# Where the SBUF tiles of a two-block transformer kernel begin: ring, activations and small tiles moved to other start addresses

## The chip, the cores and the metric

The kernel runs on one core of one Trainium2 chip. The metric is the device time of one execution in microseconds (us), the median of several runs. A core has TensorE (matmuls), VectorE, ScalarE and GpSimd, and queues that issue DMAs between HBM and the on-chip memory SBUF. SBUF has 128 partitions; a tile has one start address, the same in every partition, in bytes from the partition's beginning.

## The reference

The program computes two blocks on 256 tokens of width 2048, all in fp32. Cut to what matters:

```python
def first_block(x, ...):            # two layers
    for l in range(2):
        h = rms_norm(x, norm_g[l]); proj = h @ w_in[l]              # 2048 -> 6208
        o_a = diff_attention(q_a, k_a, v_a) ; o_a = rms_norm(o_a) * silu(z_a)
        q_b = rms_norm(c_q) @ w_uq[l]; kv = rms_norm(c_kv) @ w_ukv[l]
        o_b = mla_attention(q_b, kv, rope keys) * silu(z_b)
        x = x + concat(o_a, o_b) @ w_out[l]                         # 2048 -> 2048
    return rms_norm(x)

def second_block(x, mem, ...):      # one layer
    z = rms_norm(x) @ w_in                                          # 2048 -> 3584
    conv_out, pool_out, att = conv(z), pool(z), cross_attention(z, rms_norm(mem) @ w_kv)
    x = x + concat(conv_out, pool_out, att) @ w_out
    u = causal_dwconv(rms_norm(x) @ w_up, ffn_conv_w) + ffn_conv_b  # 2048 -> 11264
    x = x + (silu(gate) * val) @ w_down                             # 5632 -> 2048
    return rms_norm(x)
```

## The kernel before

Nearly all the work is products of a 256-token activation with large weight matrices that come from HBM once. The weights pass in 656 units of 1,024 columns per partition (512 KB; two of them per layer are half as wide) through a ring of four slots. Per unit:

- SP loads it into `stage` (`load`, L292), as soon as the remainder of the unit four before is done;
- ScalarE rounds it to fp32r, the format in which TensorE takes a matmul in one pass, into `w_hi` (`round_unit`, L299);
- VectorE writes what the rounding left, `stage - w_hi`, into `w_lo` (`rest_unit`, L304);
- TensorE multiplies with three products, high x high, high x low and low x high. Round and remainder run three units ahead of TensorE (`LEAD`).

The activations lie split in the same way, high and low half side by side, in `xT`, `mT` (attention and mixer outputs) and `act_T` (FFN).

There are two forms of product. `product_rows` (L326 to L328) holds a 128x128 block of the activation as weights in the array and streams 512 columns of `w_hi` or `w_lo`: 12 matmuls a unit, for all products but the two below. `product_cols` (L344 to L348) holds a 128x128 block of `w_hi` or `w_lo` and streams `xT`: a 256-column matmul with the low weights and a 512-column one with the high weights, 16 a unit. It serves the second block's in-projection (56 units) and the FFN's up-projection (22 turns of 8 units). The heads' transposes, scores and outputs are small fp32 matmuls in the other four PSUM banks (`aux`), written by hand in between the units. Every wait is on a semaphore; the order on each engine is the order of the code.

Where tiles lie is set by the order of their declarations alone. `sb(name, shape)` puts a tile behind the last one, its size rounded up to a multiple of 32 bytes, from address 16,512 on (16,384 bytes of DMA scratch and four constants of 32 bytes stand below). Three stacks share the upper part in time: `b1` (first block) and `b2` (second block) both start behind `bias`, and the FFN's tiles start where `mT` had started.

Of the kernel before, what the change touches and what calls it, by code (L numbers as in the profile page):

```python
# [28 lines left out]
P = 128  # L29
SEQ = 256  # L30
T = SEQ // P
D = 2048
KT = D // P
LAYERS = 2
# [3 lines left out]
HEADS = 8  # L38
# [28 lines left out]
TAPS = 3  # L67
# [28 lines left out]
FFN_ROWS = 2 * FT  # L96
# [67 lines left out]
def build(nc, dram, out):  # L164
# [12 lines left out]
    with ctx:  # L177
        def sb(name, shape, dt=F32, stack=ctx):
            return stack.enter_context(nc.sbuf_tensor("sb_" + name, shape, dt))
# [2 lines left out]
            return ctx.enter_context(nc.semaphore(name))  # L182


        ident = sb("ident", [P, P])
        par_ffn = sb("par_ffn", [P, TAPS + 1, FFN_ROWS])
        stage = sb("stage", [P, RING, UNIT])
        w_hi = sb("w_hi", [P, RING, UNIT], F32R)
        w_lo = sb("w_lo", [P, RING, UNIT], F32R)
        x = sb("x", [P, T, D])  # L190
        xT = sb("xT", [P, KT, 2, SEQ], F32R)
        par = sb("par", [P, G_ALL])
        turn_f32 = sb("turn_f32", [P, 2, 512])
        qkT = turn_f32[:, 1, :]
        sumsq_x = sb("sumsq_x", [P, T, 4])
# [2 lines left out]
        newton_v = sb("newton_v", [P, 16])  # L198
        newton_t = sb("newton_t", [P, 16])
        junk = sb("junk", [P, 512], BF16)  # L200
        sumsq_o = sb("sumsq_o", [P, HEADS * T])
        rstd_o = sb("rstd_o", [P, HEADS * T])
        sumsq_m = sb("sumsq_m", [P, T, 4])
        gain_c = sb("gain_c", [P, 8])
        neg_lam = sb("neg_lam", [P, LAYERS])


        acc = ctx.enter_context(nc.psum_tensor("acc", [P, 4, 512], F32))
# [264 lines left out]
        b1 = lambda name, shape, dt=F32: sb(name, shape, dt, block1)  # L473
# [9 lines left out]
        krT = b1("krT", [P, SEQ])  # L483
        s = b1("s", [P, 3 * SEQ])
        pT = b1("pT", [P, 3 * P])
        lam_l = b1("lam_l", [P, 1])
        neg_max = b1("neg_max", [P, 4])
        row_sum = b1("row_sum", [P, 4])
        inv_sum = b1("inv_sum", [P, 4])
        mix_f = b1("mix_f", [P, 2])  # L490
        sumsq_c = b1("sumsq_c", [P, 4])
        rstd_c = b1("rstd_c", [P, 4])
        sumsq_m2 = b1("sumsq_m2", [P, T])
        rstd_m = b1("rstd_m", [P, T])
        dots = b1("dots", [P, 2 * LAYERS])
# [45 lines left out]
        gfin = ffn_tmp[:, :, :, :].rearrange("p a c t -> p (a c t)")  # L541
        rb3 = sb("rb3", [P, T, P])
        rbc3 = sb("rbc3", [P, SEQ])
        act_T = sb("act_T", [P, FT, 2, SEQ], F32R)
        taps = sb("taps", [P, TAPS + 1, 2, 2])


        U2 = U_MEM + LAYERS * U_LAYER
# [1380 lines left out]
```

How the kernel before makes its waits and increments, by code:

```python
            def __call__(self, ins):  # L272
                self.n += 1
                ins.then_inc(self.semaphore, 1)
                self.eng.wait_ge(self.semaphore, self.base + self.n)
# [10 lines left out]
        def load(sp, base, j, src, n):  # L286
            if not (isinstance(base, int) and base + j < RING):
                sp.wait_ge(lo_ready, base + (j - RING + 1))
            k = src.shape[1]
            dst = stage[:, j % RING, 0:k * n].rearrange("p (k n) -> p k n", n=n)
            sp.dma_start(dst, src).then_inc(staged[j % RING], 16)
# [1 line left out]
        def round_unit(act, quads, j, size=UNIT):  # L294
            act.wait_ge(staged[j % RING], quads * 16 + (j // RING + 1) * 16)
            if not (isinstance(quads, int) and 4 * quads + j < RING):
                act.wait_ge(unit_used, quads * 4 + (j - RING + 1))
            act.activation(w_hi[:, j % RING, 0:size], stage[:, j % RING, 0:size], ACT.Copy).then_inc(hi_ready, 1)
# [1 line left out]
        def rest_unit(dve, base, j, size=UNIT):  # L301
            dve.wait_ge(hi_ready, base + (j + 1))
            dve.tensor_tensor(w_lo[:, j % RING, 0:size], stage[:, j % RING, 0:size],
                              w_hi[:, j % RING, 0:size].bitcast(F32), ALU.subtract).then_inc(lo_ready, 1)
# [5 lines left out]
        def product_rows(pe, base, j, lhs, k0, nk, n, pair, first, last, before_tile1=None):  # L311
            pe.wait_ge(lo_ready, base + (j + 1))
            slot = j % RING
            hi = w_hi[:, slot, 0:nk * n].rearrange("p (k n) -> p k n", n=n)
```

## Time and profile before

| | us |
|---|---|
| median of 3 runs | 2006.61 |
| lowest and highest run | 2005.53, 2006.81 |
| the profiled execution, its own time | 2005.53 |
| its span, first to last instruction | 2003.7 |

The mean granted TensorE clock of that span is 0.996. The profile's columns: PE is TensorE's matmuls, PEld its weight loads (which overlap them), DVE is VectorE, ACT ScalarE, POOL GpSimd, SP the queue that issues most loads. The ends of matmuls are modelled, so a busy TensorE is not one at its peak; the spacing of matmuls is a better measure than the length of one. Line numbers are those of the kernel before.

### The profile page before, as it was taken

The page shows a single profiled execution, that of the slowest core. Times are in us where ns is not written, and L with a number is a line of the kernel's source. Part 1 is how long each engine was busy: PE and PEld are TensorE (multiplying, and loading weights), DVE is VectorE, ACT ScalarE, POOL GpSimd, SP SyncE. Part 2 cuts the span into 40 slices and gives each one's busy share as a digit, 9 for nine tenths or more (in the row PEclk, how much of TensorE's full clock was granted, in tenths as well). Part 3 has the DMA queues.
Part 4 walks back from the last instruction along what each step waited for, and adds up shares of the span by engine and source line. Part 5 has one row for each costly group of instructions (what it writes and reads, how often), then busy time and mean ns, then how long its engine had stood idle before and what let it go on. Part 6 is the DMA issues. An engine that isn't in the chain of part 4 may idle for free.

```text
span 2003.7 us, 28710 instructions
## 1 busy us (share of the span) xinstructions
PE 1969.7 (98%) x9884; PEld 1646.0 (82%) x9884; DVE 1286.8 (64%) x1793; ACT 1028.3 (51%) x1496; POOL 46.3 (2%) x72
## 2 busy tenths in 40 slices
PE   8999999999999999999999999999999999999997
PEld 6788887888888887788888888888888888888886
DVE  6655665655654665555677775787877778754543
ACT  5533675554433565654454544555555555544442
POOL 1000003000000003000100000000000000000000
PEclk9999999999999999999999999999999999999999
DMA  8666544545566545445665545555555555565553
GB/s 282 209 191 196 149 144 130 148 148 177 177 204 191 157 149 158 145 130 186 209 192 172 166 163 189 184 184 183 188 186 186 183 188 188 185 213 191 196 191 125
DMA packets 245653, 357.36 MB, mean 178 GB/s; under 512 B 15238, under 2 KB 134368, under 8 KB 245036
## 3 DMA queue, kind: packets, MB, share of 16 engines
q1 hardware_dynamic: 243916, 349.35, 55.0%
q0 software_dynamic: 1632, 6.67, 1.0%
q8 instruction: 58, 0.95, 0.2%
q14 instruction: 47, 0.39, 0.1%
HBM read 352.82 MB, written 3.16 MB: 178 GB/s over the span
## 4 chain that ended last, share of the span: by engine, by line
PE 93%; issue 4%; POOL 2%; DVE 1%; DMA 0%; ACT 0%; SPq 0%; POOLq 0%; DVEq 0%; ACTq 0%
PE acc L348 20%; PE acc L326 18%; PE acc L328 18%; PE acc L327 18%; PE acc L347 10%; PE aux L403 2%; PE acc L344 1%; PE aux L816 1%; PE aux L815 1%; PE acc L345 1%; DMA sb_kz<-mem 0%; PE aux L778 0%; POOL sb_kz L684 0%; PE aux L797 0%; PE aux L981 0%
## 5 line engine op out<-in xcount | busy, mean ns | idle before, releaser
L304 DVE TENSOR_TENSOR sb_w_lo<-sb_stage,sb_w_hi 128x1024 fp32r<-128x1024 f32 x656 | 801.5, 1224 | 536.2 <-ACT sb_w_hi L299 528.4
L299 ACT ACTIVATE sb_w_hi<-sb_stage 128x1024 fp32r<-128x1024 f32 x656 | 690.8, 1056 | 640.9 <-PE acc L328 368.3
L348 PE MATMUL acc<-sb_xT,sb_w_hi 128*128 128x512 f32 x1740 | 616.5, 398 | 0.0
L347 PE MATMUL acc<-sb_xT,sb_w_lo 128*128 128x256 f32 x1740 | 490.2, 282 | 0.0
L348 PEld LDWEIGHTS acc<-sb_xT,sb_w_hi 128*128 128x128 f32 x1740 | 326.9, 188 | 77.3
L347 PEld LDWEIGHTS acc<-sb_xT,sb_w_lo 128*128 128x128 f32 x1740 | 328.6, 189 | 2.6
L326 PE MATMUL acc<-sb_w_hi,sb_xT 128*128 128x512 f32 x768 | 307.6, 401 | 0.9 <-issue 0.9
L327 PE MATMUL acc<-sb_w_lo,sb_xT 128*128 128x512 f32 x768 | 300.2, 391 | 0.0
L328 PE MATMUL acc<-sb_w_hi,sb_xT 128*128 128x512 f32 x768 | 300.1, 391 | 0.0
L326 PE MATMUL acc<-sb_w_hi,sb_mT 128*128 128x512 f32 x560 | 225.3, 402 | 0.0
L328 PE MATMUL acc<-sb_w_hi,sb_mT 128*128 128x512 f32 x560 | 218.9, 391 | 0.0
L327 PE MATMUL acc<-sb_w_lo,sb_mT 128*128 128x512 f32 x560 | 218.9, 391 | 0.0
L326 PEld LDWEIGHTS acc<-sb_w_hi,sb_xT 128*128 128x128 f32 x768 | 144.9, 189 | 32.1 <-issue 1.6
L328 PEld LDWEIGHTS acc<-sb_w_hi,sb_xT 128*128 128x128 f32 x768 | 144.7, 188 | 31.0
L327 PEld LDWEIGHTS acc<-sb_w_lo,sb_xT 128*128 128x128 f32 x768 | 145.0, 189 | 28.0 <-issue 0.2
L326 PE MATMUL acc<-sb_w_hi,sb_act_T 128*128 128x512 f32 x352 | 136.9, 389 | 0.0
L327 PE MATMUL acc<-sb_w_lo,sb_act_T 128*128 128x512 f32 x352 | 136.9, 389 | 0.0
L328 PE MATMUL acc<-sb_w_hi,sb_act_T 128*128 128x512 f32 x352 | 136.9, 389 | 0.0
L326 PEld LDWEIGHTS acc<-sb_w_hi,sb_mT 128*128 128x128 f32 x560 | 105.6, 189 | 23.3 <-issue 1.0
L328 PEld LDWEIGHTS acc<-sb_w_hi,sb_mT 128*128 128x128 f32 x560 | 105.4, 188 | 23.1
L327 PEld LDWEIGHTS acc<-sb_w_lo,sb_mT 128*128 128x128 f32 x560 | 105.6, 189 | 20.1
L1813 DVE SCALAR_TENSOR_TENSOR sb_ffn_tmp<-sb_ffn_tmp,sb_taps 128x254 f32<-128x254 f32 (+1 forms) x176 | 77.3, 480 | 1.6
(248 smaller groups left out, 1574.9 us busy)
## 6 DMA issues: line engine op xcount, KB each, us to landing
sb_stage<-w_in SPq DMA_DIRECT2D x248, 512.0 KB, 3.8
sb_stage<-w_up SPq DMA_DIRECT2D x176, 512.0 KB, 3.4
sb_stage<-w_out SPq DMA_DIRECT2D x96, 512.0 KB, 3.6
sb_stage<-w_down SPq DMA_DIRECT2D x88, 512.0 KB, 4.4
sb_stage<-w_kv SPq DMA_DIRECT2D x16, 512.0 KB, 6.1
sb_stage<-w_ukv SPq DMA_DIRECT2D x16, 512.0 KB, 3.5
sb_stage<-w_uq SPq DMA_DIRECT2D x12, 512.0 KB, 3.6
sb_kz<-mem SPq DMA_DIRECT2D x4, 512.0 KB, 10.4
```

Source lines behind the costliest of these rows:

```text
L299: act.activation(w_hi[:, j % RING, 0:size], stage[:, j % RING, 0:size], ACT.Copy).then_inc(hi_ready, 1)
L304: dve.tensor_tensor(w_lo[:, j % RING, 0:size], stage[:, j % RING, 0:size], w_hi[:, j % RING, 0:size].bitcast(F32), ALU.subtract).then_inc( ...
L326: pe.matmul(o, x_hi, hi[:, k, :], start=first and k == 0, stop=False)
L327: pe.matmul(o, x_hi, lo[:, k, :], start=False, stop=False)
L328: mm = pe.matmul(o, x_lo, hi[:, k, :], start=False, stop=last and k == nk - 1)
L344: pe.matmul(o, hi[:, k, cols], both, start=True, stop=False)
L345: mm = pe.matmul(o[:, 0:SEQ], lo[:, k, cols], xT[:, k0 + k, 0, :], start=False, stop=False)
L347: pe.matmul(o[:, 0:SEQ], lo[:, k, cols], xT[:, k0 + k, 0, :], start=False, stop=False)
L348: mm = pe.matmul(o, hi[:, k, cols], both, start=False, stop=last and k == 3)
L403: mm = pe.transpose(aux[:, bank, i * P:(i + 1) * P], src(i), ident[:, :])
L815: pe.matmul(o, qkT[:, q * P:(q + 1) * P], qkT[:, 2 * P:2 * P + keys], start=True, stop=False)
L1813: last = dve.scalar_tensor_tensor(out=y[:, k, d:SEQ], in0=sum3[:, k, 0:SEQ - d], scalar=taps[:, 2 - d, half, k:k + 1], in1=y[:, k, d:SEQ], ...
```

## The change

The declarations are written in another order, and five small tiles go to another stack. No instruction is added, removed or moved on any engine: engine by engine (TensorE, VectorE, ScalarE, GpSimd, SP) the rows of the two programs are the same, except that line numbers of the helpers are lower by five. What differs is the start addresses in them.

```diff
-        ident = sb("ident", [P, P])
-        par_ffn = sb("par_ffn", [P, TAPS + 1, FFN_ROWS])
         stage = sb("stage", [P, RING, UNIT])
         w_hi = sb("w_hi", [P, RING, UNIT], F32R)
         w_lo = sb("w_lo", [P, RING, UNIT], F32R)
         x = sb("x", [P, T, D])
         xT = sb("xT", [P, KT, 2, SEQ], F32R)
+        ident = sb("ident", [P, P])
         par = sb("par", [P, G_ALL])
+        par_ffn = sb("par_ffn", [P, TAPS + 1, FFN_ROWS])
         turn_f32 = sb("turn_f32", [P, 2, 512])
...
-        sumsq_o = sb("sumsq_o", [P, HEADS * T])
-        rstd_o = sb("rstd_o", [P, HEADS * T])
-        sumsq_m = sb("sumsq_m", [P, T, 4])
-        gain_c = sb("gain_c", [P, 8])
-        neg_lam = sb("neg_lam", [P, LAYERS])
...
+        neg_lam = b1("neg_lam", [P, LAYERS])
         lam_l = b1("lam_l", [P, 1])
+        gain_c = b1("gain_c", [P, 8])
...
+        sumsq_o = b1("sumsq_o", [P, HEADS * T])
+        rstd_o = b1("rstd_o", [P, HEADS * T])
...
+        sumsq_m = b1("sumsq_m", [P, T, 4])
...
+        taps = sb("taps", [P, TAPS + 1, 2, 2])
         act_T = sb("act_T", [P, FT, 2, SEQ], F32R)
-        taps = sb("taps", [P, TAPS + 1, 2, 2])
```

The start addresses that follow, each with what is left over past a multiple of 2,048 bytes:

| tile | before | past 2,048 | after | past 2,048 |
|---|---|---|---|---|
| ident | 16,512 | 128 | 114,816 | 128 |
| par_ffn | 17,024 | 640 | 115,904 | 1,216 |
| stage | 18,432 | 0 | 16,512 | 128 |
| w_hi | 34,816 | 0 | 32,896 | 128 |
| w_lo | 51,200 | 0 | 49,280 | 128 |
| x | 67,584 | 0 | 65,664 | 128 |
| xT | 83,968 | 0 | 82,048 | 128 |
| par | 116,736 | 0 | 115,328 | 640 |
| turn_f32 | 117,312 | 576 | 117,312 | 576 |
| mT, ffn_tmp | 122,880 | 0 | 122,656 | 1,824 |
| bias | 155,648 | 0 | 155,424 | 1,824 |
| qa (first tile of `b1`) | 163,840 | 0 | 163,616 | 1,824 |
| s (`b1`) | 224,288 | 1,056 | 224,064 | 832 |
| zT | 170,016 | 32 | 169,792 | 1,856 |
| mkv | 198,688 | 32 | 198,464 | 1,856 |
| mkT | 206,880 | 32 | 206,656 | 1,856 |
| act_T | 133,120 | 0 | 132,960 | 1,888 |
| taps | 223,232 | 0 | 132,896 | 1,824 |

All starts after are multiples of 32; `stage`, `w_hi`, `w_lo`, `x` and `xT` are multiples of 128, and `mT` and `act_T` are 32 past a multiple of 64. The distances among `stage`, `w_hi`, `w_lo`, `x` and `xT` stay as they were.

## Rows read from the trace of the kernel before

**Rows 1.** Page, span and busy time: us, share of the span, instructions.

```profile
span 2003.7 us, 28710 instructions
...
PE 1969.7 (98%) x9884; PEld 1646.0 (82%) x9884; DVE 1286.8 (64%) x1793; ACT 1028.3 (51%) x1496; POOL 46.3 (2%) x72
```

**Rows 2.** Page, part 4: the chain that ended last, by engine.

```profile
PE 93%; issue 4%; POOL 2%; DVE 1%; DMA 0%; ACT 0%; SPq 0%; POOLq 0%; DVEq 0%; ACTq 0%
```

**Rows 3.** Windows, two stretches: span, busy us (instructions) by engine, PEclk, DMA share, GB/s.

```profile
1355.00:1395.00 40.00, 40.00 (x229) 34.74 (x228) 30.83 (x43) 22.11 (x28) 0.00 (x0) 1.00 0.60 190
1800.00:1850.00 50.00, 50.00 (x222) 41.43 (x221) 24.52 (x23) 21.00 (x23) 0.00 (x0) 1.00 0.57 191
```

**Rows 4.** Groups by shape: busy us, mean ns | idle us before, releasers.

```profile
L304 DVE TENSOR_TENSOR sb_w_lo<-sb_stage,sb_w_hi 128x1024 fp32r<-128x1024 f32 x652 | 798.7, 1227 | 535.3 <-ACT sb_w_hi L299 528.2 <-DVE sb_rstd_m L449 0.3
L299 ACT ACTIVATE sb_w_hi<-sb_stage 128x1024 fp32r<-128x1024 f32 x652 | 688.3, 1058 | 640.9 <-PE acc L328 368.3 <-PE acc L348 267.5 <-DMA sb_stage<-w_in 3.0
...
L347 PEld LDWEIGHTS acc<-sb_xT,sb_w_lo 128*128 128x128 f32 x1740 | 328.6, 189 | 2.6
L348 PEld LDWEIGHTS acc<-sb_xT,sb_w_hi 128*128 128x128 f32 x1740 | 326.9, 188 | 77.3
L326 PE MATMUL acc<-sb_w_hi,sb_xT 128*128 128x512 f32 x768 | 307.6, 401 | 0.9 <-issue 0.9
...
L326 PE MATMUL acc<-sb_w_hi,sb_mT 128*128 128x512 f32 x560 | 225.3, 402 | 0.0
L328 PE MATMUL acc<-sb_w_hi,sb_mT 128*128 128x512 f32 x560 | 218.9, 391 | 0.0
...
L326 PE MATMUL acc<-sb_w_hi,sb_act_T 128*128 128x512 f32 x352 | 136.9, 389 | 0.0
...
L328 PE MATMUL acc<-sb_w_hi,sb_act_T 128*128 128x512 f32 x352 | 136.9, 389 | 0.0
```

**Rows 5.** Groups by shape: the small fp32 products, transposes first.

```profile
L403 PE MATMUL aux<-sb_ident,sb_x 128*128 128x128 f32 x128 | 19.1, 271 | 0.0
...
L778 PE MATMUL aux<-sb_ident,sb_s 128*128 128x128 f32 x96 | 15.6, 271 | 0.0
...
L815 PE MATMUL aux<-sb_turn_f 128*128 128x256 f32 x32 | 9.5, 380 | 0.0
...
L999 PE MATMUL aux<-sb_mkT,sb_zT 128*128 128x256 f32 x16 | 4.1, 379 | 0.0
```

**Rows 6.** Groups by shape, VectorE: product with a broadcast row.

```profile
L1805 DVE TENSOR_TENSOR sb_ffn_tmp<-sb_ffn_tmp,sb_rbc 128x512 f32<-128x512 f32 x44 | 30.5, 692 | 1.5
...
L1713 DVE TENSOR_TENSOR sb_zT<-sb_sum,sb_rbc 128x512 f32<-128x512 f32 x9 | 6.2, 692 | 0.3
```

**Rows 7.** DMA issues: KB each, median us from issue to landing.

```profile
sb_stage<-w_up SPq DMA_DIRECT2D x176, 512.0 KB, 3.4
sb_stage<-w_out SPq DMA_DIRECT2D x96, 512.0 KB, 3.6
sb_stage<-w_down SPq DMA_DIRECT2D x88, 512.0 KB, 4.4
...
mem_kv<-sb_qa POOLq DMA_DIRECT2D x1, 1024.0 KB, 5.2
...
sb_mkv<-mem_kv POOLq DMA_DIRECT2D x1, 1024.0 KB, 5.4
```

**Rows 8.** Timeline, one turn of the ring: start us, us, instruction, idle before.

```profile
500.82 1.23 DVE L304 TENSOR_TENSOR sb_w_lo<-sb_stage,sb_w_hi 128x1024 fp32r<-128x1024 f32 x1 [1.43 <-ACT sb_w_hi L299]
...
502.21 3.09 SPq L292 DMA_DIRECT2D sb_stage<-w_out  x2
...
510.61 1.06 ACT L299 ACTIVATE sb_w_hi<-sb_stage 128x1024 fp32r<-128x1024 f32 x1 [0.29 <-PE acc L328]
```

**Rows 9.** Waits: engine and line, what for, us in total, times, longest.

```profile
ACT sb_w_hi L299 <- DMA sb_stage<-w_in: 3.0, 1, 3.0
```

**Rows 10.** The chain in order of time, its start: start us, us, what.

```profile
2.53 9.67 DMA sb_kz<-mem
```

## Prediction

> **What bounds the kernel now.** I read the page's busy times first, then the chain of waits, then two steady stretches by window, then the groups of instructions by shape, and last the waits and the loads. TensorE is busy for 1969.7 of 2003.7 us, 98%, against 64% for VectorE and 51% for ScalarE [rows 1], and it carries 93% of the chain that ended last [rows 2]. So the time is, nearly, the number of matmuls times the spacing between them. The two steady stretches show that spacing [rows 3]: in the FFN's up-projection 229 matmuls in 40 us, 175 ns each or 349 ns for a pair of one 256-column and one 512-column product; in the down-projection 222 in 50 us, 225 ns each. The granted clock is 1.00 in both, the upper of its two levels.
>
> This change adds, removes and moves no instruction. It moves tiles in SBUF. The question is therefore one: does a stream, a weight load, a vector or scalar pass or a transfer take longer or shorter from another start address? The rows of before can answer part of it, because this kernel already has tiles at awkward starts: ident stands at 16,512 (128 bytes past a multiple of 2,048, where the ring goes), s at 224,288, zT at 170,016 and mkv at 198,688, each 32 bytes past a multiple of 64, while x, xT, mT, act_T, ffn_tmp and the ring stand at multiples of 2,048.
>
> **The change part by part.**
>
> TensorE, 8,752 large matmuls. 5,040 of them are product_rows (L326 to L328: 768 + 560 + 352 rows of each of three lines [rows 4]); there the moving operand is w_hi or w_lo, whose starts go from a multiple of 2,048 to 128 bytes past one, and the weights are xT (the same shift), mT and act_T (to 32 bytes past a multiple of 64). 3,712 are product_cols: 232 units (56 of the in-projection, 176 of the FFN) of 16. There w_hi and w_lo are the weights and xT moves. What does the address cost? Compare like with like [rows 5]. A 128x256 matmul on turn_f32, a multiple of 64, takes 380 ns (L815); on mkT and zT, both 32 bytes past a multiple of 64, 379 ns (L999). A transpose of x, a multiple of 2,048, takes 271 ns; of s, 271 ns (L778); both read ident at 128 past a multiple. The differences are 0 and -1 ns. These are fp32 products and not the fp32r of the large ones, and the ends of matmuls are modelled, so I take them as the nearest rows and not as proof. The value I take is 0 ns. The ends: one ns either way is what such rows can't tell, -8.8 to +8.8 us over 8,752; upward I keep 7 ns on the row products as well, worked out under the slower rival, +35 us.
>
> Weight loads. They run beside the matmuls. For 1740 pairs of product_cols the two loads take 189 + 188 ns and the load side sat idle for 77.3 + 2.6 us, 46 ns a pair [rows 4]. A load that grows by less than 23 ns disappears there. In product_rows the load of 188 or 189 ns stands in a spacing of 225 ns, so 36 ns cover it. Cost 0, and the cover is those two numbers.
>
> VectorE and ScalarE. The round to w_hi (1058 ns) and the remainder (1227 ns) follow one another within a unit, and in the down-projection a unit of 12 matmuls lasts 12 x 225 = 2.7 us, so neither is near its limit; the two sat idle for 535 and 641 us before these instructions [rows 4]. From rows, the address costs them nothing either: the same 128x512 product with a broadcast row takes 692 ns into ffn_tmp at a multiple of 2,048 and 692 ns into zT at 32 past a multiple of 64 [rows 6]. Even 10% on both, 0.23 us a unit, would be covered by the ring, whose remainder is made three units ahead of its use. Cost 0.
>
> The loads. Each 512 KB load writes rows of 2 KB (1 KB for the narrow units) to a start that was a multiple of 2,048 and is now 128 past one. Landing takes 3.4 us for w_up [rows 7]. How much is spare is read from one turn of the ring [rows 8]: VectorE's remainder ends at 500.82 + 1.23 = 502.05, the load into that slot goes out at 502.21, and ScalarE rounds it four units on, at 510.61: 8.4 us, while a w_out load lands in 3.6 us [rows 7], under half of it. In all the run ScalarE waited once for a stage load, 3.0 us [rows 9]. From one row on the other side: the load into mkv, at an odd start, lands in 5.4 us, and the store of the same 1024 KB from qa, at a multiple of 2,048, in 5.2 [rows 7]. So steady transfers cost 0; what remains is the opening, where the chain rests for 9.67 us on the load of mem [rows 10]. I give it +0.2 us (the 4% between 5.4 and 5.2 on half of 9.67 us, the rest being latency); the ends are 0 and +2 us, the latter if all of the 9.67 us grew by a fifth, which is how far loads of one size already differ (w_down lands in 4.4 us, w_out in 3.6 [rows 7]).
>
> The Trainium skill has a rule that speaks against the change. "DMA: Bandwidth & Descriptors", section "How a descriptor splits into AXI transactions", says that a descriptor is cut at every 256 bytes, that one which starts off such a boundary begins with a partly used transaction, and gives the beats. It speaks of reads; if it held for the SBUF side of a load as well, a 2 KB row at 128 past a boundary would by that page need 9 transactions and 68 beats in place of 8 and 64, a 1 KB row 36 in place of 32. By that rule, and as an estimate from the page's beats, loads would take 6 to 12% longer. No row here shows a 2 KB row at such a start, so the trace neither agrees nor disagrees. On the rows above it would make the opening about 1 us longer and leave the rest covered, 2008 us, which is still no change, so it has no chance of its own.
>
> Small tiles (par, par_ffn, taps, the sums and the rstd values) are read by instructions of some 160 to 690 ns on engines that have idle time. Cost 0.
>
> The sum: 0 (TensorE) + 0 (loads of weights) + 0 (VectorE, ScalarE) + 0.2 (opening) on a span of 2003.7 and an execution of 2005.53, thus 2005.7 for the profiled execution. The median of the runs stands 1.1 above that execution, so the forecast is 2006.8 us for the median: no change.
>
> **The rivals.**
>
> Slower, because TensorE's moving rows no longer begin on a boundary. The place is product_rows. A 512-column row of 2 KB is 32 pieces of 64 bytes; if a start 128 bytes off costs one piece more, each of 5,040 matmuls takes 225/32 = 7 ns more, 35 us, and the time is 2042. It decides from 0.8 ns a matmul on, since 5,040 x 0.8 is 4 us. The column products would gain nothing and lose nothing: one eighth of a 512-byte weight row is 24 ns a load, 47 a pair, against the 46 of cover. For it speaks that the row products are the tightest loop and that their fp32r streams have no row at an odd start. Against it: rows 5, and the transposes in particular, which read ident at the very offset in question. Chance 8%.
>
> Slower, because the queues run full. The DMA share is 0.60 and 0.57 in the two steady stretches [rows 3]. Loads bind the kernel only when packets take 1/0.60 = 1.67 times as long. If writes off a boundary took twice as long, the shares would be 1.20 and 1.14, and most of the run would stretch by 10 to 20%: some 2250 us. Short of that there is the mild form, a few us at the opening and at changes of stage, 2011 to 2015, where a fifth more on each load is no longer covered at four or five of them. Together 5%.
>
> Faster, because a clash of equal starts goes. If two operands that begin at the same place in a 2,048-byte frame disturbed one another, moving them apart would help. xT and w_hi keep their distance of 49,152 bytes, so nothing changes there. mT against w_hi goes from 88,064 (a multiple of 2,048) to 89,760 (not one). L326 on mT takes 402 ns and on act_T 389; L328 391 and 389 [rows 4]. If that were such a clash, 13 x 560 + 2 x 2 x 560 = 9.5 us would come back: 1997. Against it: act_T has the same residue and has no such excess, and xT has it at 401. The likelier reason is the work of the attention heads between those units. Chance 4%.
>
> **How the numbers follow.** No change 83% (its own range 2004.5 to 2009.5), TensorE slower 8%, loads slower 5%, faster 4%. A difference under 0.2%, 4 us, is about what a measurement of this kernel can't tell from no change. Same takes 0.83, faster 0.04, slower the 8 and the 5, 0.13. The range for eight in ten: down to 2003.5, where a little of the faster case begins, and up to 2012, which takes in the mild form of slower loads and 0.6 ns on every large matmul (5.2 us); the 2042 stays out.
>
> **What would show it.** Right: the matmul counts of the two windows within one of 229 and 222, the group means of L326 to L328, L347 and L348 within 1 ns, L304 and L299 within 5 ns, w_up landing in 3.4 to 3.8 us, and the first transposes at about 12.2 us. The TensorE rival would show as a spacing above 226 ns in the down-projection, where nothing else disturbs it; the transfer rival as a higher DMA share, longer landings and more waits of ScalarE on stage; the faster one as L326 on mT falling to 389 ns. The forecast is wrong if the median leaves 2002.6 to 2010.8.

## The result and the profile after

The kernel after takes 2022.12 us, the median of four runs (2021.78 to 2022.82), against 2006.71 before. The ratio is 1.008, 95% interval 1.0067 to 1.0093: 15.4 us slower, outside the predicted range, and on the side that had been given 13%.

The page of after, its span and busy times:

```profile
span 2020.8 us, 28710 instructions
...
PE 1987.9 (98%) x9884; PEld 1648.1 (82%) x9884; DVE 1288.4 (64%) x1793; ACT 1028.2 (51%) x1496; POOL 46.3 (2%) x72
```

TensorE is busy 18.2 us longer (1987.9 against 1969.7 [rows 1]), the span is 17.1 us longer, and the chain by engine reads as in [rows 2]. So the time is not a wait; the same matmuls take longer. The two stretches of [rows 3], ten and fifteen microseconds later in this run:

```profile
1365.00:1405.00 40.00, 40.00 (x229) 34.76 (x228) 30.86 (x43) 22.14 (x28) 0.00 (x0) 1.00 0.61 190
1815.00:1865.00 50.00, 50.00 (x216) 40.20 (x215) 24.44 (x22) 20.10 (x22) 0.00 (x0) 1.00 0.58 189
```

The up-projection still has 229 matmuls in 40 us. The down-projection has 216 in 50 us where it had 222. Which matmuls pay is read from the groups by shape (busy us, mean ns, idle before); they answer to [rows 4], and each line number is five lower:

```profile
L299 DVE TENSOR_TENSOR sb_w_lo<-sb_stage,sb_w_hi 128x1024 fp32r<-128x1024 f32 x652 | 797.6, 1226 | 547.3 <-ACT sb_w_hi L294 540.4 <-DVE sb_rstd_m L444 0.3
L294 ACT ACTIVATE sb_w_hi<-sb_stage 128x1024 fp32r<-128x1024 f32 x652 | 688.4, 1058 | 653.0 <-PE acc L323 381.1 <-PE acc L343 268.8 <-DMA sb_stage<-w_kv 1.5
L343 PE MATMUL acc<-sb_xT,sb_w_hi 128*128 128x512 f32 x1740 | 616.4, 398 | 0.0
L342 PE MATMUL acc<-sb_xT,sb_w_lo 128*128 128x256 f32 x1740 | 490.9, 282 | 0.0
L342 PEld LDWEIGHTS acc<-sb_xT,sb_w_lo 128*128 128x128 f32 x1740 | 328.7, 189 | 2.6
L343 PEld LDWEIGHTS acc<-sb_xT,sb_w_hi 128*128 128x128 f32 x1740 | 327.6, 188 | 76.7
L321 PE MATMUL acc<-sb_w_hi,sb_xT 128*128 128x512 f32 x768 | 308.9, 402 | 0.0
...
L321 PE MATMUL acc<-sb_w_hi,sb_mT 128*128 128x512 f32 x560 | 227.7, 407 | 0.0
L322 PE MATMUL acc<-sb_w_lo,sb_mT 128*128 128x512 f32 x560 | 222.5, 397 | 0.0
L323 PE MATMUL acc<-sb_w_hi,sb_mT 128*128 128x512 f32 x560 | 222.3, 397 | 0.0
...
L321 PE MATMUL acc<-sb_w_hi,sb_act_T 128*128 128x512 f32 x352 | 139.2, 395 | 0.0
L323 PE MATMUL acc<-sb_w_hi,sb_act_T 128*128 128x512 f32 x352 | 139.2, 395 | 0.0
```

The row products on mT and act_T grew, 402 to 407, 391 to 397 and 389 to 395 ns. Those on xT grew by 1 ns. The column products' loads are unchanged, and so are their matmuls, which in before read:

```profile
L348 PE MATMUL acc<-sb_xT,sb_w_hi 128*128 128x512 f32 x1740 | 616.5, 398 | 0.0
L347 PE MATMUL acc<-sb_xT,sb_w_lo 128*128 128x256 f32 x1740 | 490.2, 282 | 0.0
```

In busy time mT gives 2.4 + 3.6 + 3.4 = 9.4 us (L322 was L327, which stood at 218.9 before, as L328 did), act_T 3 x 2.3 = 6.9 us, and xT about 1 us a line, 3 us: 19 us, a little over the 18.2 of the page. The spacing from one start to the next, which needs no modelled end, closes better. In the trace it went from 226.7 to 233.3 ns on act_T, from 228.0 to 233.4 on mT and from 227.4 to 227.9 on xT: 1056 x 6.6 + 1680 x 5.4 + 2304 x 0.5 = 17.2 us, the whole of the 17.1 by which the span grew. The weight loads are as long as before, 188 or 189 ns. VectorE's remainder went from 1227 to 1226 ns, ScalarE's rounding stayed at 1058.

The rows on which the prediction had rested moved by 1 ns at most ([rows 5] are 271, 271, 380 and 379):

```profile
L398 PE MATMUL aux<-sb_ident,sb_x 128*128 128x128 f32 x128 | 19.2, 272 | 0.0
...
L778 PE MATMUL aux<-sb_ident,sb_s 128*128 128x128 f32 x96 | 15.7, 272 | 0.0
...
L815 PE MATMUL aux<-sb_turn_f 128*128 128x256 f32 x32 | 9.6, 380 | 0.0
...
L999 PE MATMUL aux<-sb_mkT,sb_zT 128*128 128x256 f32 x16 | 4.1, 380 | 0.0
```

Nor did the transfers matter. Landings (median us) and the opening wait, for [rows 7] and [rows 10]:

```profile
sb_stage<-w_up SPq DMA_DIRECT2D x176, 512.0 KB, 3.6
sb_stage<-w_out SPq DMA_DIRECT2D x96, 512.0 KB, 3.7
sb_stage<-w_down SPq DMA_DIRECT2D x88, 512.0 KB, 4.4
```

```profile
2.53 9.88 DMA sb_kz<-mem
```

The opening costs 0.2 us more, as forecast, but single profiles can't bear that out: in the seven kernels below in which the tile of this load stands where it stood in before, the same piece takes 9.38 to 9.84 us. w_up lands 0.2 us later, under cover, and it does so in x32 too, where the ring stands still (3.6). The Trainium skill's "DMA: Bandwidth & Descriptors", section "How a descriptor splits into AXI transactions", would by its beats have made loads 6 to 12% longer, if it held for writes into SBUF. The trace doesn't agree: the median packet of the ring's rows takes 84 ns (2 KB) and 46 ns (1 KB) in before and in after, and in b_ring128, with the ring at +128 as well, the means are 102.0 and 51.6 ns against 102.7 and 51.6 in before. After's own means, 104.2 and 52.5, are no higher than those of x32, 104.9 and 53.2.

### The profile page after: what moved, and what is told of

Read it like the earlier page. It is cut to its first block, busy times and chain, and to the rows that moved or that the text cites. A ratio compares the mean times of both kernels' runs of the same rounds, so it can differ in the third digit from the quotient of the medians.

```text
span 2020.8 us, 28710 instructions
## 1 busy us (share of the span) xinstructions
PE 1987.9 (98%) x9884; PEld 1648.1 (82%) x9884; DVE 1288.4 (64%) x1793; ACT 1028.2 (51%) x1496; POOL 46.3 (2%) x72
## 4 chain that ended last, share of the span: by engine, by line
PE 93%; issue 4%; POOL 2%; DVE 1%; DMA 0%; ACT 0%; SPq 0%; POOLq 0%; DVEq 0%; ACTq 0%
PE acc L343 20%; PE acc L321 18%; PE acc L322 18%; PE acc L323 18%; PE acc L342 10%; PE aux L398 2%; PE acc L339 1%; PE aux L816 1%; PE aux L815 1%; PE acc L340 1%; DMA sb_kz<-mem 0%; PE aux L778 0%; PE aux L797 0%; POOL sb_kz L686 0%; PE aux L981 0%
## 5 line engine op out<-in xcount | busy, mean ns | idle before, releaser
L294 ACT ACTIVATE sb_w_hi<-sb_stage 128x1024 fp32r<-128x1024 f32 x656 | 691.0, 1056 | 653.0 <-PE acc L323 381.1
L322 PE MATMUL acc<-sb_w_lo,sb_xT 128*128 128x512 f32 x768 | 301.0, 392 | 0.0
L321 PE MATMUL acc<-sb_w_hi,sb_mT 128*128 128x512 f32 x560 | 227.7, 407 | 0.0
L322 PE MATMUL acc<-sb_w_lo,sb_mT 128*128 128x512 f32 x560 | 222.5, 397 | 0.0
L323 PE MATMUL acc<-sb_w_hi,sb_mT 128*128 128x512 f32 x560 | 222.3, 397 | 0.0
L322 PEld LDWEIGHTS acc<-sb_w_lo,sb_xT 128*128 128x128 f32 x768 | 145.4, 189 | 28.3 <-issue 0.2
L321 PE MATMUL acc<-sb_w_hi,sb_act_T 128*128 128x512 f32 x352 | 139.2, 395 | 0.0
L323 PE MATMUL acc<-sb_w_hi,sb_act_T 128*128 128x512 f32 x352 | 139.2, 395 | 0.0
L322 PE MATMUL acc<-sb_w_lo,sb_act_T 128*128 128x512 f32 x352 | 139.2, 395 | 0.0
L322 PEld LDWEIGHTS acc<-sb_w_lo,sb_mT 128*128 128x128 f32 x560 | 105.9, 189 | 23.0
L323 PEld LDWEIGHTS acc<-sb_w_hi,sb_act_T 128*128 128x128 f32 x352 | 66.0, 188 | 16.1
```

The lines of the kernel that those rows point to most:

```text
L294: act.activation(w_hi[:, j % RING, 0:size], stage[:, j % RING, 0:size], ACT.Copy).then_inc(hi_ready, 1)
L321: pe.matmul(o, x_hi, hi[:, k, :], start=first and k == 0, stop=False)
L322: pe.matmul(o, x_hi, lo[:, k, :], start=False, stop=False)
L323: mm = pe.matmul(o, x_lo, hi[:, k, :], start=False, stop=last and k == nk - 1)
```

## The experiments

What is common to the slow groups? mT and act_T moved against the ring, and xT did not. I call distance the start of the tile that holds the weights minus the start of the tile that is streamed, modulo 256 bytes. All weight blocks and all streamed rows begin at multiples of 512 bytes within their tiles, and w_hi and w_lo are 16,384 bytes apart, so one number serves a whole product. In before every distance is 0. In after it is 160 for mT, 224 for act_T and 0 for xT. In the column products xT is the stream; for them the text and the tables give by how much the stream is moved up.

Four kernels ran first. Where a window is shown, it is a steady stretch of the down-projection (row products on act_T), 50 us, to be held against 222 matmuls in [rows 3].

**b_up32 and b_up64: before, with mT, act_T and all above moved.**

```diff
+        pad_m = sb("pad_m", [P, 8], F32, mixing)     # 32 bytes; [P, 16] in b_up64
         mT = sb("mT", [P, KT, 2, SEQ], F32R, mixing)
...
+        pad_f = sb("pad_f", [P, 8])
         ffn_tmp = sb("ffn_tmp", [P, 4, 2, SEQ])
```

> The kernel before with 32 bytes of padding below mT and below ffn_tmp, so that mT, act_T and all tiles above begin 32 bytes past their old starts (mT and act_T 32 past a multiple of 64); ring, x and xT stay at multiples of 2,048. Theory A (a 128x128 weight block that begins off a multiple of 64 bytes costs TensorE about 6 ns in the row products): row products on act_T and mT 6 ns slower, those on xT unchanged, 1056 x 6.7 + 1680 x 5.5 = 16 us, so 2022 us. Theory B (the clash is between equal places in a 2,048-byte frame, any shift between weights and stream counts): the same 2022, only the next run parts them. Theory C (the moving rows of the ring at +128 cost it): no change, 2007.

> The same with 64 bytes: mT and act_T at 64 past a multiple of 2,048, so a multiple of 64 but not of 128 or more. Theory A: no change, 2007 us, act_T matmuls 389 ns by the groups. Theory B: as slow as after, 2020 to 2022.

Measured: 2022.37 us, ratio 1.0081 (1.0064 to 1.0098), and 2022.62 us, ratio 1.0080 (1.0063 to 1.0097). In b_up32 and then in b_up64:

```profile
1805.00:1855.00 50.00, 50.00 (x216) 40.22 (x216) 24.44 (x22) 20.05 (x23) 0.00 (x0) 1.00 0.57 189
```

```profile
1805.00:1855.00 50.00, 50.00 (x216) 40.30 (x215) 24.07 (x23) 20.45 (x22) 0.00 (x0) 1.00 0.56 187
```

Both at 216 (by the starts in the trace 233.3 ns apart in both, 226.7 in before). Theory A, a penalty for weight tiles off a multiple of 64, falls with b_up64. Theory C, a penalty for the ring's start, falls with both, since the ring stood where it had stood.

**b_ring128: ring, x, xT and the small tiles as in after; mT and all above as in before.**

```diff
-        ident = sb("ident", [P, P])
-        par_ffn = sb("par_ffn", [P, TAPS + 1, FFN_ROWS])
         stage = sb("stage", [P, RING, UNIT])
...
         xT = sb("xT", [P, KT, 2, SEQ], F32R)
+        ident = sb("ident", [P, P])
         par = sb("par", [P, G_ALL])
+        par_ffn = sb("par_ffn", [P, TAPS + 1, FFN_ROWS])
```

> Order of declarations of after for ident, the ring, x, xT, par and par_ffn (these at +128 past multiples of 2,048), but the sums stay below mT, so mT, act_T and all above stand where they stood before. Theory A: 2007, at most 2 us above (the 0.8 ns seen on the xT row products of after). Theory C: 2022. Theory B: 2022 too, since the distance from w_hi to mT changes.

Measured: 2020.44 us, ratio 1.0074 (1.0057 to 1.0090).

```profile
1805.00:1855.00 50.00, 50.00 (x217) 40.54 (x216) 24.46 (x22) 20.24 (x23) 0.00 (x0) 1.00 0.57 189
```

mT and act_T are back at multiples of 2,048 and still slow; the distance is now 128.

**a_up32: after, with the edit of b_up32 (32 bytes below mT and below ffn_tmp).**

> The kernel after with 32 bytes of padding below mT and below ffn_tmp: mT at 122,688 and act_T at 132,992, multiples of 64 but of nothing larger, all else as after. Theory A: the loss is gone, 2007 to 2009. Theory B: still 2022.

Measured: 2008.13 us, ratio 1.0010 (1.0001 to 1.0020). The down-projection, and the row products on mT by shape:

```profile
1805.00:1855.00 50.00, 50.00 (x222) 41.38 (x222) 24.46 (x22) 21.37 (x23) 0.00 (x0) 1.00 0.56 190
```

```profile
L321 PE MATMUL acc<-sb_w_hi,sb_mT 128*128 128x512 f32 x560 | 226.5, 404 | 0.0
L323 PE MATMUL acc<-sb_w_hi,sb_mT 128*128 128x512 f32 x560 | 220.4, 394 | 0.0
```

Thirty-two bytes took 14 of the 15 us back, which theory A had forecast for the wrong reason. The distance of act_T is 0 here (100,096 = 391 x 256), and 222 matmuls fit again. mT stands at 192, and its groups lie in between, 404 and 394 ns. Theory B, the distance in a frame of 2,048 bytes, is out: there act_T's distance is 1,792, and it is fast. What fits all is theory D: distance modulo 256, 0 being fast.

**a_same: after, every large tile 128 past a multiple of 256, so all distances 0.**

```diff
+        pad_m = sb("pad_m", [P, 24], F32, mixing)
...
+        pad_f = sb("pad_f", [P, 24])
...
+        pad_a = sb("pad_a", [P, 48])      # below act_T
```

> The kernel after with padding (96 bytes below mT and below ffn_tmp, 192 more below act_T) so that ring, x, xT, mT and act_T all begin 128 past a multiple of 256: every absolute start is off, every distance from a stream in the ring to its weights is a multiple of 256. Theory D (what counts is the distance of weight tile and stream modulo 256 bytes; at 0 the row products are spaced 226.7 ns, at the other distances seen so far 230 to 234): all row products at 227, 2006 us. Rival E (absolute starts count in some other way, and the fast act_T of the last run was chance): some row products stay at 230 or more, over 2010.

Measured: 2007.62 us, ratio 1.0002 (0.9992 to 1.0012). The change's loss is gone though every one of these tiles still starts off a multiple of 256.

```profile
1805.00:1855.00 50.00, 50.00 (x223) 41.39 (x222) 24.47 (x22) 21.10 (x23) 0.00 (x0) 1.00 0.60 191
```

**x32 and x128: before with xT alone moved, 32 or 128 bytes.** Small tiles go to `b1` so that mT stays.

```diff
+        pad_x = sb("pad_x", [P, 8])       # [P, 32] in x128
         xT = sb("xT", [P, KT, 2, SEQ], F32R)
...
-        neg_lam = sb("neg_lam", [P, LAYERS])          # x128: sumsq_o and rstd_o instead
+        neg_lam = b1("neg_lam", [P, LAYERS])
```

> The kernel before with xT alone 32 bytes up (neg_lam moves to b1 so that mT and all above stand where they stood). Theory D: row products on xT, 2304 of them, go from 227 to 233 ns, 2304 x 6 = 14 us, those on mT and act_T stay; in the column products the distance of weights (w_hi, w_lo) and stream (xT) changes too, and if the same holds there, up to 1856 pairs x 2 x 6 = 22 us more or less, sign open. Time 2020 if the column products don't care. Rival E: no change on xT, since after had xT at 128 without loss.

> The same with xT 128 bytes up. Theory D: rows on xT at 230 to 234 ns, 2016 to 2022. A modulus of 128 in place of 256 would leave it at 2006; the kernel with the ring at +128 and mT at 0 speaks against that.

Measured: x32 2010.13 us, ratio 1.0019 (1.0010 to 1.0029); x128 2016.12 us, ratio 1.0045 (1.0029 to 1.0062). In x32, the row products by shape and the up-projection's window:

```profile
L326 PE MATMUL acc<-sb_w_hi,sb_xT 128*128 128x512 f32 x768 | 311.9, 406 | 0.2 <-issue 0.2
...
L326 PE MATMUL acc<-sb_w_hi,sb_mT 128*128 128x512 f32 x560 | 225.1, 402 | 0.0
```

```profile
1355.00:1395.00 40.00, 40.00 (x232) 35.41 (x232) 32.84 (x48) 22.88 (x28) 0.00 (x0) 1.00 0.61 188
```

Rows on xT went from 401 to 406 ns and those on mT stayed at 402, as theory D has it. The surprise stands in the window: 232 matmuls in 40 us where 229 had been. Here w_hi and w_lo are the weights and xT is the stream. By the starts in the trace an ordinary column unit, eight pairs, takes 2773 ns in x32 and 2824 in before, 346.7 and 353 ns a pair. So before's equal starts, best for rows, were not best for columns. In x128 the row products are spaced 232.3 ns on xT and 228.0 on mT, which speaks for 256 and against 128 as the modulus; a column pair takes 350.9 ns in the mean, against 352.2 in before.

**scan1: before with xT 64 and mT 96 bytes up, and act_T 272, which is 16 past a multiple of 256; a single run.**

> The kernel before with xT 64, mT 96 and act_T 16 bytes up. For the spacings alone: theory D has all three kinds of row product between 229 and 236 ns; were 16 bytes (four columns of fp32) too little to matter, act_T would stay at 227. Time about 2035.

Measured: 2029.64 us. By the starts in the trace the row products are spaced 233.3 ns on xT, 234.1 on mT and 233.3 on act_T. Sixteen bytes were enough here.

```diff
+        pad_x = sb("pad_x", [P, 16])              # 64 bytes, below xT
...
+        pad_m = sb("pad_m", [P, 8], F32, mixing)  # 32 more, below mT
...
+        pad_f = sb("pad_f", [P, 8])               # the same below ffn_tmp
...
+        pad_a = sb("pad_a", [P, 40])              # 160 more, below act_T
+        act_all = sb("act_all", [P, FT * 2 * SEQ + 8], F32R)
+        act_T = act_all[:, 4:4 + FT * 2 * SEQ].rearrange("p (a c t) -> p a c t", a=FT, c=2)
```

**micro: TensorE alone.** The program has one line for each group of 120 matmuls. Cut down, with d and s for the bytes by which weights and stream are moved, a row group reads:

```python
for i in range(120): pe.matmul(acc[:, i // 3 % 2, :], wt[:, d // 4 + i // 2 % 8 * P : ...], (lo if i % 3 == 1 else hi)[:, s // 4 + ...], ...)
```

> The disputed cost by itself: a program that leaves out the whole computation (it returns x unchanged) and has TensorE alone run groups of 120 matmuls from SBUF tiles, with VectorE, ScalarE and the queues idle. Row groups (512-column streams, a weight load each) with the weights 0, 16, 32, 64, 96, 128, 160, 192, 224, 256 and 384 bytes up against the stream, then both 32 up, both 128 up, and the stream alone 32 up; column groups (512 and 256 columns in turn) with the stream 0 to 256 bytes up against the weights. Theory D: rows at 0, 256, 32+32 and 128+128 spaced 227 ns, all others 229 to 236; columns fastest at 32. Rival (the loss needs the other engines or DMAs, which read and write the same tiles in the kernel): all groups at 227 and all pairs alike.

The next lines show what the trace says of four row groups (duration min/median/max, first and last start): distances 0, 32 and 192, then both tiles 32 up. They count the 80 matmuls that stream `hi`, the first and the last of the 120 among them.

```profile
L208 PE MATMUL acc<-sb_hi,sb_wt x80: 389/389/389, 41.3 to 68.3; 128*128 128x512 f32 x80
```

```profile
L210 PE MATMUL acc<-sb_hi,sb_wt x80: 392/395/397, 95.7 to 123.5; 128*128 128x512 f32 x80
```

```profile
L215 PE MATMUL acc<-sb_hi,sb_wt x80: 388/390/394, 235.7 to 262.9; 128*128 128x512 f32 x80
```

```profile
L219 PE MATMUL acc<-sb_hi,sb_wt x80: 387/389/397, 346.3 to 373.3; 128*128 128x512 f32 x80
```

From first to last start there are 119 spacings: 27.0 us or 227 ns at 0, 27.8 us or 234 at 32, 27.2 us or 229 at 192, and 27.0 us again with both 32 up. All groups, from the starts in the trace:

| distance of weights, rows | 0 | 16 | 32 | 64 | 96 | 128 | 160 | 192 | 224 | 256 | 32+32 | 128+128 |
|---|---|---|---|---|---|---|---|---|---|---|---|---|
| ns a matmul | 226.7 | 226.7 | 233.3 | 233.3 | 234.3 | 232.4 | 233.3 | 228.9 | 233.3 | 226.7 | 226.7 | 226.7 |

| stream moved, columns | 0 | 16 | 32 | 64 | 96 | 128 | 160 | 192 | 224 | 256 |
|---|---|---|---|---|---|---|---|---|---|---|
| ns a pair | 353.4 | 346.7 | 346.7 | 353.4 | 350.0 | 351.1 | 346.7 | 353.3 | 353.5 | 353.4 |

Weights 384 up gave 232.4 ns, as 128 did, and columns with both tiles 32 up 353.4, as at 0. No other engine was at work, and the DMA engines were busy 1% of the time, so the rival falls: TensorE alone is enough. The table also repeats the kernels: 160 and 224 (after's mT and act_T) are 233.4 and 233.3 ns there, 128 (b_ring128's act_T) 232.4, 192 (a_up32's mT) 229.2. Within whole units that nothing interrupts a_up32's mT stands at 228.8, and before's mT at 226.7 like act_T.

**micro2 and x16: the beat.** Sixteen bytes, slow in scan1, were fast here.

> TensorE alone again (the computation is left out, x comes back unchanged), the weight blocks now in the kernel's order and each group of 120 preceded by 12 slow matmuls at distance 128, so that no group inherits the beat of a fast one. Rows with the weights 0, 4, 8, 12, 16, 20, 24, 240, 248 and 32 bytes up; columns with the stream 0, 4, 8, 12, 16, 20, 24, 240 and 32 up. If the distance alone decides: 16 stays at 227 as in the first such run. If the beat is inherited (16 bytes gave 233 in the kernel and 227 behind a fast group): 0 returns to 227 by itself, 16 stays at 233.

micro2 was read for two row groups written alike, weights 16 up, each behind 12 matmuls at distance 128; before those the first has groups at distances of 4, 8 and 12 bytes, the second a group at distance 0:

```profile
L216 PE MATMUL acc<-sb_hi,sb_wt x80: 392/396/398, 163.6 to 191.4; 128*128 128x512 f32 x80
```

```profile
L230 PE MATMUL acc<-sb_hi,sb_wt x80: 389/389/396, 377.5 to 404.5; 128*128 128x512 f32 x80
```

The first needs 27.8 us for its 119 spacings, 233 ns, the second 27.0 us, 227 ns. The two groups are the same code at the same addresses, and what ran before is all that differs. So at 16 bytes the pace isn't set by the distance alone; that it is inherited from the group before is the likely reading, and then the 12 matmuls at distance 128 didn't wipe it out. Distance 0 came to 226.7 behind such a group too. Distances 4 to 24 and 240 to 248 gave 228 to 233 ns in the rows. In the columns 12, 16 and 32 gave 346.7, 8 and 240 gave 353.4, but 4 gave 360 and 20 and 24 gave 356, and distance 0, at 353.4 in micro, now ran at 346.6: columns at equal starts have two paces as well, and the kernels showed only the slower.

```diff
-        xT = sb("xT", [P, KT, 2, SEQ], F32R)
+        xT_all = sb("xT", [P, KT * 2 * SEQ + 8], F32R)
+        xT = xT_all[:, 4:4 + KT * 2 * SEQ].rearrange("p (k h t) -> p k h t", k=KT, h=2)
...
```

> The kernel before with xT alone 16 bytes up. By the first isolated run (rows with weights 16 up 226.7, columns with the stream 16 up 346.7 a pair against 353.4): the 1856 pairs gain 6.7 ns each, 12 us, and the 2304 row products on xT cost nothing: 1995 us. If a distance of 16 keeps whatever beat it finds, as act_T did 16 up in the kernel: rows on xT at 233, +14 us, net 2009.

Measured: 2002.85 us, ratio 0.9976 (0.9966 to 0.9986), between the two forecasts. Columns run at 346.7; of the row units on xT some run at 227 throughout and some at 233, 230.2 in the mean. Of the 120 such units that nothing interrupts 66 are fast and 54 slow, none in between, and they come in long stretches, 44 fast ones in a row and later 46 slow ones. Both paces of one distance, in one kernel, and each is kept from unit to unit.

**wlo32: w_lo alone 32 bytes off; a single run.**

> The kernel before with w_lo alone 32 bytes off (it stands behind xT now). Of three row matmuls one (the middle line, L327 of before) streams w_lo. Theory D, if the cost comes from the stream that runs while the next weights are loaded: one of three spacings grows by some 6 ns, or two of three by 3; row total + 5040/3 x 6 = 10 us. In the column products the weights of the 256-column matmul move. If all row products went to 233 as in after (+16 us), the distance between the two streams would count too.

```diff
-        w_lo = sb("w_lo", [P, RING, UNIT], F32R)
         x = sb("x", [P, T, D])
         xT = sb("xT", [P, KT, 2, SEQ], F32R)
+        pad_l = sb("pad_l", [P, 8])
+        w_lo = sb("w_lo", [P, RING, UNIT], F32R)
...
```

Measured: 2019.47 us. Row spacings went from 226.7 to 231.7 ns on act_T, 227.4 to 232.5 on xT and 228.0 to 231.5 on mT: 1056 x 5.0 + 2304 x 5.1 + 1680 x 3.5 = 23 us, more than either forecast for the rows (10 and 16 us), though one stream of three is off. A column unit gained, 2818 to 2782 ns in the mean, x 232 = 8 us. The net of 15 us is the 14 us of the span. Where all three streams of a row product are off, act_T's cost 6.6 ns each, here 5.0. That a third of the streams costs most of the whole says that the matmuls of a row product don't pay one by one; how they share it stays open.

**ffn32 and col32: what beats both.** Rows want equal starts, columns the stream 32 bytes up, and the second block reads xT only in column products. So the activation is written 32 bytes higher for them, in the same tile.

```diff
-        xT = sb("xT", [P, KT, 2, SEQ], F32R)
+        xT_all = sb("xT", [P, KT * 2 * SEQ + 8], F32R)
+        xT_view = lambda e: xT_all[:, e:e + KT * 2 * SEQ].rearrange("p (k h t) -> p k h t", k=KT, h=2)
+        xT, xT_ffn = xT_view(0), xT_view(8)
...
-                            product_cols(pe, turn_ * U_FFN + U3, 4 * half + i, 4 * i, half, i == 0, i == 3)
+                            product_cols(pe, turn_ * U_FFN + U3, 4 * half + i, 4 * i, half, i == 0, i == 3, xT_ffn)
# col32 besides: the in-projection, and at the end of the layer loop
+            flat = xT_all[:, bass.ds(layer * 8 + 4 * c * 2 * SEQ, 4 * 2 * SEQ)]
```

> The kernel before, but the normalized activation of the FFN is written 32 bytes above where xT stands for the layers (same tile, 32 bytes longer, neg_lam in b1 to make room), so that the layers' row products keep distance 0 and the 176 units of FFN column products get distance 32. Theory D, with the pair measured at 346.7 ns with xT 32 bytes up against 353: 1408 pairs x 6.3 = 8.9 us less, 1998 us, and nothing changed elsewhere. Rival: the gain of the column products in that other run came with its slower row products (another pace of the ring), then 2007.

> As ffn32, and the second block's in-projection too reads its activation 32 bytes up (its first three parts are written at the end of the layer loop, at an address that the layer number sets), so all 232 units of column products have distance 32 and all row products distance 0. Theory (distance 0 is fast for rows, distance 32 for columns): 56 x 8 = 448 pairs more at 6.7 ns, 3 us under ffn32's 1999.7: 1996.7. If the heads' small matmuls, which break up these units, spoil the beat there, it stays at 1999.7.

Measured: ffn32 1999.73 us, ratio 0.9959 (0.9946 to 0.9973); col32 1997.55 us, ratio 0.9951 (0.9938 to 0.9965). The two windows of col32, up-projection and down-projection:

```profile
1355.00:1395.00 40.00, 40.00 (x232) 35.42 (x232) 31.52 (x46) 23.51 (x29) 0.00 (x0) 1.00 0.61 187
1805.00:1855.00 50.00, 50.00 (x222) 41.43 (x221) 24.27 (x21) 20.42 (x22) 0.00 (x0) 1.00 0.62 197
```

232 and 222: the columns' faster pace and the rows' fast one together. col32 is 9 us under before and 25 under after. Of ffn32's expected 8.9 us 7.3 came. From the start of the first FFN column unit to that of the last it is 495.9 us in before and 488.5 in ffn32, so these units hold the whole gain. Ordinary units gained 51 ns each (2824 to 2773), but the first one of an output tile, whose first two matmuls stand in the other order, only 20 (2806 to 2787), which is where most of the rest is. That col32 is faster than ffn32 is likely (3 us forecast, 2.2 found) but within their intervals.

## Why the prediction was wrong

- **TensorE, 8,752 large matmuls at 0 ns.** This is the step that failed. The measured cost was 5 to 7 ns on the 2,736 row products on mT and act_T, 16 us by starts as by busy time, and 1 us by starts (3 by busy time) around xT's. The column products kept their 0. The nearest rows [rows 5] were taken from fp32 products that compare one tile's start with another's. They could not show it, for two reasons. The cost depends on no tile's own start. And the small products don't pay for a distance either: that between x and ident went from 128 to 0, and the transposes from 271 to 272 ns. The band of one ns either way was drawn from them as well, so it was too narrow for the large ones.
- **The slower rival** had the right place (row products) and sign, but the wrong cause. It put the cost on streams at +128. Those whose weights are xT, both at +128, cost 1 ns, so that its 35 us were 20 too many; b_up32 and b_up64 lose all with the ring unmoved. That its 7 ns a matmul come near the measured 6.6 is luck: they are one piece of 64 bytes in 32, and a start moved by 128 bytes cuts no such piece.
- **The faster rival** had asked about the distance between weights and stream and dismissed it as a possible gain. Distance was the right variable, though in a frame of 256 bytes and with the other sign: equal starts are the best for rows and, in the kernel, among the slower for columns. The 402 ns on mT against 389 on act_T were no clash, as the rival's own counterargument said: within whole units before's mT runs at the same 226.7 ns. The diff's own table showed that xT kept its distance and mT did not.
- **Weight loads.** Their length was right, 188 and 189 ns, and the cover was beside the point: the spacing grew without the load growing. The Trainium skill, "SBUF — State Buffer", section "Who interferes with whom", gives TensorE two independent read ports, one for the stream and one for the weights, and says that it never waits on anyone. If that means that stream and weight load don't affect one another, micro disagrees: 226.7 against 233.3 ns by nothing but their starts, with no other engine at work. Whether ports, banks or something else couple them no run shows.
- **VectorE and ScalarE, small tiles, steady transfers 0; opening 0.2 us.** Nothing contradicts the zeros: 1226 and 1058 ns, landings within 0.2 us. The opening's 9.88 against 9.67 hits the number, but kernels that leave that tile in place differ by more, and the 5.4 us of the load into mkv, from which the 4% were drawn, is 5.3 to 5.6 there: a hit that nothing supports. The 1 KB rows are those of the 232 column units, not of the narrow ones alone (118,784 packets of 1 KB in the trace of before); the term is 0 either way.
- **The spacings** of 225 and 349 ns were read from counts that take in matmuls cut by a window's ends; by starts they are 226.7 and 353. No term hangs on the difference.
- **What would show it** was well chosen: the 222 matmuls became 216 and the 389 ns 395. Only the cause named beside them was wrong.

Shown: the loss comes from the distance modulo 256 (a_same undoes it, b_up32, b_up64 and b_ring128 bring it about, micro has it alone). Open: what in TensorE or SBUF makes it so, why some distances have two paces, and the half ns on xT's rows (227.4 to 227.9 by starts). That half ns isn't the same effect: of the 120 units on xT that nothing interrupts 118 still run at 226.7 in after, and b_up32, with ring and xT in place, has it too (228.0). It arises between such units.

## What to carry to other kernels

When TensorE runs one matmul behind another with a weight load under each, as these fp32r products do, count a steady stretch's matmuls and compare layouts by that count. For each product take the start of the weights minus the start of the stream; a few bytes of padding set it. Try distance 0 for long streams and a few others where two stream lengths alternate, and use one layout per stage where a tile serves both. And when a change is only of addresses, look for rows in which the distance between two operands differs, not only their own starts.

## What the runs showed of the hardware

- 128x512 fp32r matmuls with a weight load each: 226.7 ns apart when weights and stream start at the same place modulo 256 bytes, 229 to 234 at the other multiples of 32, with nothing else running.
- Pairs of 512 and 256 columns: 346.7 ns with the stream 32 bytes up; with equal starts 353 in the kernel, 353.4 in micro and 346.6 in micro2.
- One distance can have two paces: the same code 16 bytes apart ran at 226.7 and 233.3 ns in micro2, and in x16 whole stretches of units keep the one or the other.
- Loads into a ring 128 bytes past a multiple of 2,048: the median packet stays at 84 ns (2 KB) and 46 ns (1 KB).
- The shifted starts changed the mean of the large VectorE and ScalarE groups by 1 ns at most (1227 to 1226, 1058 to 1058).
